# A two-layer hybrid decoder: the mixers' input projected un-normed, 1/rms applied where the slabs are drained

## The reference, cut to what matters

```python
def rms_norm(x, g):
    y = x * rsqrt(mean(x * x, axis=-1, keepdims=True) + 1e-6)
    return y * g
for l in range(DEPTH):
    h = rms_norm(x, norm_mix[l])
    x = x + hybrid_mixer(h, w_in[l], w_out[l], ...)   # split_cols(h @ w_in) feeds three mixers
    h = rms_norm(x, norm_ffn[l])
    x = x + peer_ffn(h, ...)                          # 8 heads x 16 rows of peer_u and peer_v per token
return rms_norm(x, norm_final)
```

## Time and profile before

| | |
|---|---|
| median of 3 runs | 3553.36 us (3552.85 to 3555.71) |
| the profiled execution | 3554.43 us, its span 3552.6 us |
| busy: TensorE / VectorE / ScalarE / GpSimd | 81% / 62% / 21% / 34% of the span |
| projections and mixers | about 0 to 430 and 1780 to 2200 us |
| expert stages | about 430 to 1780 and 2200 to 3545 us |
| moved by DMA | 1243.73 MB, mean 350 GB/s |

### The profile page before, as it was taken

One profiled execution on the slowest core, in us unless ns is written; L12 is line 12 of the kernel. 1 busy time (PEld: TensorE's weight loads), 2 busy tenths in 40 slices (PEclk: granted clock), 3 DMA queues, 4 the chain that ended last, 5 costly groups with the idle time before them and its releaser, 6 DMA issues.

```text
span 3552.6 us, 31376 instructions
## 1 busy us (share of the span) xinstructions
PE 2862.2 (81%) x10451; PEld 1655.6 (47%) x10451; DVE 2199.6 (62%) x3084; ACT 758.4 (21%) x1195; POOL 1219.7 (34%) x1028
## 2 busy tenths in 40 slices
PE   7999948877787788777789999478778878887776
PEld 7888833423342343222388887334234323432322
DVE  6775576565665656555566655765666556655655
ACT  4354411111111111111143544111111111111111
POOL 0000065444444444444400000644444444444442
PEclk9999969999999999999999999799999999999999
DMA  5445599999999999999944454999999999999998
GB/s 192 137 151 165 179 362 420 419 421 421 421 420 422 421 420 411 422 420 419 399 144 137 146 191 153 397 420 419 421 421 421 420 422 421 416 415 422 416 421 341
DMA packets 239647, 1243.73 MB, mean 350 GB/s; under 512 B 24680, under 2 KB 33072, under 8 KB 107440
## 3 DMA queue, kind: packets, MB, share of 16 engines
q0 software_dynamic: 147456, 1073.81, 73.0%
q1 hardware_dynamic: 92080, 168.51, 14.0%
HBM read 1240.14 MB, written 2.10 MB: 350 GB/s over the span
## 4 chain that ended last, share of the span: by engine, by line
DMA 47%; PE 37%; DVE 6%; issue 5%; DVEq 2%; ACT 1%; POOL 1%; SPq 0%; POOLq 0%; ACTq 0%
DMA work<-in_peer_v_dram,idx_v 43%; PE PS L508 17%; PE PS L859 17%; DMA work<-in_peer_u_dram,idx_u 4%; DVE work L1880 2%; DVE xs L1906 1%; POOL work L1252 1%; DVEq L1496 1%; ACT hi L936 1%; DVE lo L1385 1%; PE PS L628 1%; PE PS L606 0%; PE PS L618 0%; DMA gain<-in_w_in_dram 0%; PE PS L794 0%
## 5 line engine op out<-in xcount | busy, mean ns | idle before, releaser
L859 PE MATMUL PS<-work,diag 128*128 128x512 f32 x3968 | 1861.4, 617 | 620.4 <-DMA work<-in_peer_v_dram,idx_v 454.5
L1880 DVE CUSTOM_DVE_ANT_0 work<-work,hn 128x2048 f32<-128x2048 f32 x512 | 1170.3, 2292 | 829.4 <-DMA work<-in_peer_u_dram,idx_u 817.6
L859 PEld LDWEIGHTS PS<-work,diag 128*128 128x128 f32 x3968 | 742.0, 195 | 1710.2 <-issue 1346.0
L1252 POOL DMA_INDIRECT work<-in_peer_u_dram,idx_u x512 | 649.9, 1269 | 1165.1 <-DVEq L1852 896.0
L1252 POOL DMA_INDIRECT work<-in_peer_v_dram,idx_v x512 | 569.6, 1113 | 1136.6 <-PE PS L859 1017.7
L1183 ACT ACTIVATE diag<-cst,act_k 128x128 f32<-128x128 f32 x496 | 185.5, 397 | 1219.9 <-PE PS L859 1209.9
L508 PE MATMUL PS<-hT_hi,hi 128*128 128x256 f32 x960 | 287.6, 300 | 24.5 <-DVE lo L1724 14.1
L508 PE MATMUL PS<-hi,hT_hi 128*128 128x512 f32 (+1 forms) x704 | 276.0, 392 | 3.7 <-DVE lo L1385 3.7
L508 PE MATMUL PS<-hT_lo,hi 128*128 128x256 f32 x960 | 275.7, 287 | 0.0
L508 PE MATMUL PS<-hT_hi,lo 128*128 128x256 f32 x960 | 275.5, 287 | 0.0
L508 PE MATMUL PS<-hi,hT_lo 128*128 128x512 f32 (+1 forms) x704 | 269.6, 383 | 0.0
(11 more groups left out here) (264 smaller groups left out, 1700.5 us busy)
## 6 DMA issues: line engine op xcount, KB each, us to landing
raw<-in_w_in_dram SPq DMA_DIRECT2D x40, 1024.0 KB
gain<-in_w_in_dram SPq DMA_DIRECT2D x38, 1024.0 KB, 5.0
raw<-in_peer_query_dram SPq DMA_DIRECT2D x24, 1024.0 KB
raw<-in_w_out_dram SPq DMA_DIRECT2D x16, 1024.0 KB
gain<-in_w_out_dram SPq DMA_DIRECT2D x16, 1024.0 KB, 5.1
work<-in_peer_query_dram SPq DMA_DIRECT2D x8, 1024.0 KB, 7.7
work<-in_peer_u_dram,idx_u POOLq DMA_INDIRECT x512, 11.6
work<-in_peer_v_dram,idx_v POOLq DMA_INDIRECT x512
```

The costliest lines, as they stand in the source:

```text
L859: mm = pe.matmul(PS[:, j, :], diag[:, n % RING, :], vrow[n % RING][:, j * 512:(j + 1) * 512], start=(k == 0), stop=(k == (TOPK - 2 if last ...
L1252: pool.indirect_dma_start(out=dst, out_offset=None, in_=tables[table], in_offset=bass.IndirectOffsetOnAxis(ap=idx, axis=0)).then_inc(loade ...
L1880: dve.tensor_tensor_reduce(r, r, hn[:, b, :], 1.0, 0.0, ALU.mult, ALU.add, pre[:, b, k:k + 1]).then_inc(u_free.sem, 1)
```

## The change

hn is no longer the normed input but tokens times gain, without 1/rms (`weigh_inputs`), so that it can be turned before the sums of squares are known. Since the projection is linear in each token, 1/rms enters at the drain. Slabs whose tokens lie on partitions (kv, q, ih, vm, gh, om) get it as ScalarE's scale, one activation for each block of tokens in place of one for both. Slabs whose tokens lie along the free axis (fh, qh, qkm0, qkm1) are multiplied by a row of 1/rms on VectorE (`scale_rows`); fh and qh then go through ScalarE's sigmoids and silu in place. For the row, VectorE makes two diagonals (`lay_rstd`), TensorE spreads them over all partitions by two matmuls after piece 2 (`spread_rstd`), and ScalarE copies the result out.

Tiles are turned ahead of the piece that needs them: piece p waits for tile 4 + p alone, tiles 4 and 5 are turned before piece 0, tiles 6 and 7 before piece 1, and the convolution weights after piece 1. In layer 0 SP issues the gain first, block 0 of the tokens in halves, then block 1, and piece 1 ahead of the constants and small loads. Between the layers tiles 0 to 3 are turned one of TensorE's rows earlier, block 1 is weighed slab by slab behind each part of `take_last_sum`, and the splits of pieces 1 and 2 come ahead of tiles 6 and 7 and of the root. After the last layer the final norm is as before.

The diff, cut (the end of the program, the new wait before a slab's first piece, and the remaining drains, which change as kv does, are left out):

```diff
+ROWS_SCALED = ["fh", "qh", "qkm0", "qkm1"]
+DRAINED = [name for name, _, _ in SLABS if name not in ("qkm0", "qkm1")]
+ND = len(DRAINED)
...
+            sp.dma_start(gain[:].unsqueeze(1), layer_of(norm_mix, 0).partition_broadcast(P)).then_inc(gain_loaded.sem, 16)
+            for i in range(2):
+                half = slice(i * D // 2, (i + 1) * D // 2)
+                sp.dma_start(xs[:, 0, half], x[0, 0:P, half]).then_inc(x_loaded[i].sem, 16)
+            sp.dma_start(xs[:, 1, :], x[0, P:SEQ, :]).then_inc(x_loaded[2].sem, 16)
...
-                stop_until(sp, "sp", vidx_ready.sem, vidx_ready.upto(l, 0))
-                sp.dma_start(gain[:].unsqueeze(1), layer_of(norm_mix, l).partition_broadcast(P)).then_inc(gain_loaded.sem, 16)
+                if l > 0:
+                    stop_until(sp, "sp", vidx_ready.sem, vidx_ready.upto(l, 0))
+                    sp.dma_start(gain[:].unsqueeze(1), layer_of(norm_mix, l).partition_broadcast(P)).then_inc(gain_loaded.sem, 16)
...
                 load_piece(0)
                 if l == 0:
+                    sp.wait_ge(turned.sem, turned.upto(l, 4))
+                    load_piece(1)
...
                 load_piece(2)
-                stop_until(sp, "sp", turned.sem, turned.upto(l, 4))
-                load_piece(1)
+                if l > 0:
+                    stop_until(sp, "sp", turned.sem, turned.upto(l, 4))
+                    load_piece(1)
...
+                def spread_rstd():
+
+                    pe.wait_ge(rstd_diag.sem, rstd_diag.upto(l, 1))
+                    for b in range(NB):
+                        mm = pe.matmul(PS[:, 6, b * P:(b + 1) * P], ones[:], diag[:, b, :], start=True, stop=True)
+                    mm.then_inc(rstd_spread.sem, 1)
...
-                for f in range(4, 8):
-                    turn_mix(l, f)
-                pe.wait_ge(turned_dve.sem, turned_dve.upto(l, 8))
-                if l == 0:
-                    pe.wait_ge(consts_loaded.sem, 16)
+                def conv_step():
+                    pe.wait_ge(turned_dve.sem, turned_dve.upto(l, 8))
+                    conv_weights()
+
+                steps[0] = nothing
+                steps[1] = conv_step
+                steps[2] = spread_rstd
                 for p in range(IN_PIECES):
+                    if p < 2:
+                        for f in range(4 + 2 * p, 6 + 2 * p):
+                            turn_mix(l, f)
+                    if p < 4:
+
+                        pe.wait_ge(turned_dve.sem, turned_dve.upto(l, 5 + p))
+                    if l == 0 and p == 8:
+                        pe.wait_ge(consts_loaded.sem, 16)
                     if p % 4 == 0 and p >= 8:
-
-                        pe.wait_ge(drained.sem, drained.upto(l, p // 4 - 1))
+                        slab_free(p // 4 - 2)
                     project(l, p)
                     steps.get(p, nothing)()
...
-                    if l + 1 < DEPTH and k in (6, 8, 10, 12):
-                        turn_mix(l + 1, (k - 6) // 2)
+                    if l + 1 < DEPTH and k in (4, 6, 8, 10):
+                        turn_mix(l + 1, (k - 4) // 2)
...
+            def square_sums(l, b):
+
+                if l == 0:
+                    for i in ((0, 1) if b == 0 else (2,)):
+                        act.wait_ge(x_loaded[i].sem, 16)
+                if b == 0 or l == 0:
+                    unread = squares[:, b, :] if l == 0 else lo[1][:].bitcast(F32R)
+                    a = act.activation(unread, xs[:, b, :], ACT.Square, accum_out=ss[:, b:b + 1])
+                else:
+                    for o in range(NO):
+                        act.wait_ge(x1_final.sem, x1_final.upto(l - 1, o + 1))
+                        a = act.activation(squares[:, 1, o * 512:(o + 1) * 512], xs[:, b, o * 512:(o + 1) * 512], ACT.Square,
+                                           accum_out=ssq[:, b, o:o + 1])
+                a.then_inc(sumsq_ready.sem, 1)
+
+            def root(stage):
+
+                act.wait_ge(var_ready.sem, stage)
+                act.activation(rms[:], ss[:], ACT.Sqrt).then_inc(std_ready.sem, 1)
...
+            take_mix(0, range(5))
             round_piece(0, 0)
-            take_mix(0, range(8))
+            take_mix(0, range(5, 6))
+            square_sums(0, 0)
+            square_sums(0, 1)
+            round_piece(0, 1)
+            take_mix(0, range(6, 8))
+            root(1)
+            round_piece(0, 2)
...
+                    both = lambda f: [f(b) for b in range(NB)][-1]
+                    if name in ROWS_SCALED:
+                        act.wait_ge(scaled.sem, scaled.upto(l, ROWS_SCALED.index(name) + 1))
                     if name == "fh":
-                        act.activation(cum, pt, ACT.Sigmoid)
-                        a = act.activation(kk, pt, ACT.Sigmoid, scale=-1.0)
+                        act.activation(kk, cum, ACT.Sigmoid, scale=-1.0)
+                        a = act.activation(cum, cum, ACT.Sigmoid)
                     elif name == "qh":
-                        a = act.activation(silq, pt, ACT.Silu)
+                        a = act.activation(silq, silq, ACT.Silu)
                     elif name in ("qa0", "qa1"):
                         c = 512 * int(name[2])
-                        a = act.activation(qraw[:, :, c:c + 512], p, ACT.Copy)
+                        a = both(lambda b: act.activation(qraw[:, b, c:c + 512], p[:, b, :], ACT.Copy, scale=rstd[:, b:b + 1]))
                     elif name == "kv":
-                        act.activation(gnat[:], p[:, :, 256:256 + 2 * NH], ACT.Copy)
-                        a = act.activation(kvraw, p[:, :, 0:256], ACT.Copy)
-                    elif name in ("qkm0", "qkm1"):
-                        m = 4 * int(name[3])
-                        a = act.activation(cin[:, m:m + 4, :], pt, ACT.Copy)
...
+                round_to(5)
+                act.wait_ge(rstd_spread.sem, rstd_spread.upto(l, 1))
+                act.activation(rstd_row, PS[:, 6, 0:SEQ], ACT.Copy).then_inc(rstd_laid.sem, 1)
                 drain(0)
...
+                    act.activation(rms[:], ones[:, 0:NB], ACT.Sqrt)
+                    act.wait_ge(x0_final.sem, x0_final.upto(l, 1))
+                    square_sums(l + 1, 0)
+                    diagonals(HEADS - 1, 1, range(8, TOPK, 2), last=True)
+                    take_mix(l + 1, range(6))
                     round_piece(l + 1, 1)
+                    round_piece(l + 1, 2)
+                    take_mix(l + 1, range(6, 8))
+                    square_sums(l + 1, 1)
+                    root(var_ready.upto(l, 2))
...
+            def weigh_inputs(l, b, o, n):
+
+                cols = slice(o * n, (o + 1) * n)
+                dve.tensor_tensor(hn[:, b, cols], xs[:, b, cols], gain[:, cols], ALU.mult).then_inc(normed.sem, 1)
+
+            def lay_rstd():
+
+                for b in range(NB):
+                    d = dve.tensor_scalar(diag[:, b, :], ident, rstd[:, b:b + 1], None, ALU.mult)
+                d.then_inc(rstd_diag.sem, 1)
...
+            dve.wait_ge(gain_loaded.sem, gain_loaded.upto(0, 16))
+            for o in range(2):
+                dve.wait_ge(x_loaded[o].sem, 16)
+                weigh_inputs(0, 0, o, D // 2)
+            take_mix(0, range(2))
+            dve.wait_ge(x_loaded[2].sem, 16)
+            weigh_inputs(0, 1, 0, 512)
+            take_mix(0, range(2, 4))
+            weigh_inputs(0, 1, 1, 512)
+            take_mix(0, range(4, 5))
+            split_piece(0, 0)
+            take_mix(0, range(5, 6))
+            weigh_inputs(0, 1, 2, 512)
+            weigh_inputs(0, 1, 3, 512)
+            dve.drain().then_inc(gain_used.sem, 1)
+            split_piece(0, 1)
+            take_mix(0, range(6, 8))
+            variance(None, 2)
             invert(None, 1)
-            normalise(0, 0)
-            normalise(0, 1)
-            take_mix(0, range(4))
-            split_piece(0, 0)
-            take_mix(0, range(4, 8))
+            lay_rstd()
+            split_piece(0, 2)
...
+                def scale_rows(name, dst):
+
+                    j = [n for n, _, _ in SLABS].index(name)
+                    dve.wait_ge(pieces_used.sem, pieces_used.upto(l, 4 * (j + 1)))
+                    dve.tensor_tensor(dst, pair(j).rearrange("p b (m t) -> p (b m) t", m=2),
+                                      bc(rstd_row.unsqueeze(1), [P, 4, SEQ]), ALU.mult).then_inc(scaled.sem, 1)
+                    dve.drain()
...
                 split_to(6)
+                dve.wait_ge(rstd_laid.sem, rstd_laid.upto(l, 1))
+                scale_rows("fh", cum)
...
-                split_to(9)
+                split_to(10)
+                scale_rows("qh", silq)
                 dve.wait_ge(drained.sem, drained.upto(l, 2))
-                split_to(10)
...
+                scale_rows("qkm0", cin[:, 0:4, :])
                 soft(0)
                 for n in range(NBATCH):
                     take_probs(n)
                     if n + 1 < NBATCH:
                         soft(n + 1)
```

(79 more changed lines are left out.)

89 lines of the change are left out of this document (47 added, 42 removed).

## The result

The changed kernel takes 3567.07 us (median of 7 runs, 3565.75 to 3568.05), the kernel before, run beside it, 3555.16 (7 runs). The ratio is 1.0034, 95% interval 1.0024 to 1.0043: 12 us slower, where the prediction said 3555.7 and no change. The profiled execution has a span of 3565.3 us, against the 3552.6 of the earlier trace rows.

A forecast was written before the change was run, and what follows sets the result against it. Up to and in the recurrence's levels, the chain VectorE and ScalarE share sets the time, not the products. Layer 0 summed to 0.0 and layer 1 to +2.3: 3553.36 + 2.3 = 3555.7 us, range 3549.5 to 3560.

The forecast's parts named there:

- Start of layer 0: Layer 0's projection start: first product at 18.8 against 24.82; with added TensorE work, -5.6 us at the end of fh.
- Between the layers: From last expert row to layer 1's projection: first product 5.7 us earlier, -3.3 at the end of fh after added costs.
- x: Delay of the last expert row by piece 1's earlier load: between 0 and 2.7 us, taken as +1.2.
- The fh and qh drains: VectorE's row products ahead of ScalarE's drains: first level weights +4.8 us after fh, taken as +4.6 in each layer.
- costed at nothing: Row products on qkm slabs, 1.22 us each, and remaining doubled drains: free where TensorE is never idle.
- Drains by scale: ScalarE's kv and q drains, two activations for one: 1.2 us each instead of 0.6 and 0.9, +1.0 per layer.
- The rival of the clock: In the recurrence's levels, gaps make TensorE's clock fall again: +6 on top of +2.3, 3561.7 us; chance 0.12.
- rival that the start's gain stands: Up to the levels TensorE's queue is last, hiding fh and qh products: -8.5, 3544.9 us; chance 0.15.

The follow-up runs named there:

- before, a wait that is always met: Kernel before, with a second wait on ScalarE's own finished rounding added after TensorE's wait, ahead of its fh and qh drains: 3555.53 us.
- before, load on TensorE's wait: Kernel before, with an always-met second wait written ahead of TensorE's wait at fh and qh, so the table load carries TensorE's wait: 3560.89 us.
- one wait: Changed kernel, with ScalarE waiting at fh and qh for VectorE's row product alone, its wait for TensorE removed: 3559.83 us.
- waits swapped: Changed kernel, with ScalarE's two waits before fh and qh kept but in the other order, so the table load carries TensorE's wait: 3559.43 us.
- product first: Changed kernel, with VectorE multiplying fh and qh by the row of 1/rms before it splits pieces 5 and 9: 3560.52 us.
- four repairs: Changed kernel, with ScalarE's TensorE wait dropped, row products before splits, turns two rows later, and layer 0's piece 0 rounded and split before tile 4: 3554.13 us.
- fh and qh unscaled: Changed kernel, with 1/rms left out of fh and qh, which ScalarE takes straight from PSUM as in the kernel before: 3552.13 us.
- run with the later turns: Changed kernel, with tiles 0 to 3 turned between the layers two rows later again, as in the kernel before: 3566.58 us.

## Why the prediction was wrong

*Start of layer 0: mechanism right, size off by 1.5.* First product at 20.28, not 18.8. The prediction kept piece 0's rounding at 14.55, because four 1 MB blocks lie ahead of it in both orders; it began at 15.91. Of these 1.4, the transfer of piece 0 is 0.8 (15.35 above, when nothing stands in front) and tile 4's rounding on ScalarE about 0.6.

*Between the layers: right.* -5.8 for -5.7, and x was 1.22 for 1.2, in all runs with the early turns. By the rule of the Trainium skill ("DMA: Bandwidth & Descriptors", Queues, rings and completion order), which I had read as giving 2.7 here, the load would have had its full share before the last row; the row shows less than half of that.

*The fh and qh drains: the step that failed.* It priced them at +4.8 by the first weights; measured is 34.0 - 26.5 = +7.5. The difference of 2.7 is twice the 1.28 load. The step counted the exponential's load as "in series", because the trace of before shows it there, and left those of sigmoid and silu at nothing, because there they lay in idle time. They aren't in its list "costed at nothing" either, where the cover would have had to be named: the load was free as long as nothing made it wait for VectorE. With the table loads repaired the step holds. End of fh to first weights, in both layers:

```
before                               26.5
before, a wait that is always met    26.5
before, load on TensorE's wait       27.8
after, in two executions             34.0
one wait                             31.3
waits swapped                        31.3
product first                        30.6
four repairs                         28.3
fh and qh unscaled                   26.5
```

Loads out of the open: 2.7 (2 x 1.28 = 2.56). Product first: 3.4 (2.29 + 1.25 = 3.54). Both and no more: 5.7 (6.1). After with hidden loads against fh and qh unscaled: 4.8, where the sum had 4.8. TensorE's waits ahead of pieces 7 and 8 in layer 1 are 1.75 and 1.46 after, for 0.9 and 1.6 predicted; with the loads hidden they are 0.86 and 1.46.

*Drains by scale: mechanism right, a little too dear.* kv and the gates' columns take 1.0 up to the next rounding (1882.99 to 1884.00) and q 1.14 (1909.72 to 1910.86), where the prediction had 1.2 for each. Before, the same stretches took 0.54 and 0.91, so the rows say +0.7 per layer for the predicted +1.0, and the levels, in which both drains stand, are longer by 1.0 and 0.7 in the two layers. The run without them gained 3.4 us over two layers; the intervals leave both 2.0 and 1.4 open.

*The rival of the clock* (0.12): the clock fell more often, but the levels aren't longer by it. Table by stretches, the levels of layer 1 before, then the 22 us ahead of them and the levels after (window, length, busy PE, PEld, DVE, ACT, POOL, granted clock, DMA share, GB/s):

```profile
1845.96:1909.96 64.00, 59.93 (x341) 51.98 (x340) 42.84 (x45) 24.84 (x21) 0.00 (x0) 0.95 0.45 148
```
```profile
1824.86:1846.86 22.00, 18.59 (x151) 18.01 (x151) 15.88 (x23) 10.58 (x9) 0.00 (x0) 1.00 0.27 77
1846.86:1910.86 64.00, 57.78 (x329) 51.30 (x328) 39.28 (x43) 27.14 (x26) 0.00 (x0) 0.91 0.46 149
```

The 22 us ahead of the levels have gaps of 3.4 in all, the waits ahead of pieces 7 and 8 among them. The levels behind have a granted clock of 0.91 instead of 0.95. One minus the clock times the length is the work, at full speed, that the lower clock takes away. Summed over the levels and the 20 us behind them in both layers it is 11.8 to 12.2 in the three executions with the change's drains as they are, 8.4 without the factor on kv and q, 3.8 with one wait, 8.3 with the waits swapped, and 5.2 to 7.0 in the three of the kernel before and its variants. So TensorE lost some 6 us more to 1.2 instead of 2.4 GHz. The time from the first to the last level's weights doesn't follow: it is 62.5 and 63.0 in the two layers after, 62.2 and 64.2 with one wait, which has the smallest loss of these, and without the factor on kv and q 61.7 and 62.1, as short as before (61.6 and 62.3) at a larger loss. In the levels VectorE and ScalarE's chain ends last, as the prediction said, and a slower TensorE beside it cost nothing that these traces show. So the clock doesn't explain why the medians give back 8.1 and 8.5 with one wait and with swapped waits where the timeline gives back 5.3 (2.7 in each layer); that difference of about 3 is what the intervals leave open.

*The sum.* Predicted +2.3, the table loads +5.1, the start of layer 0 +1.5: 8.9 of 12. Most of the rest, 2.7 in the profiled executions, lies behind the levels, where the prediction had nothing. Of it, 0.95 is shown: in layer 1 ScalarE idles 6.71 instead of 5.46 for a load of w_out, and TensorE idles for the split behind it, 0.95 in this execution, 0.58 to 1.08 in all ten traces of the changed kernel and its variants and not at all in the three of the kernel before and its variants. What causes the remainder stays open; that stretch differs by up to 4.8 between traces (290.0 to 294.8 in layer 0). The rival that the start's gain stands fell with the row-first run: the chain and not TensorE's queue is last. The chance of 0.12 for slower was too low: the range's upper end counted the drains' chain at most 5 in each layer, and a bound for work that is inserted into a wait should have held every instruction that can be pushed behind that wait.

## What to carry to other kernels

When a drain gets a new producer, list everything that stood in the idle time ahead of it, table loads included, and ask of each which wait it will carry. If an activation needs two waits and a table, look at the compiled order: write last the wait that is met first, or drop the one that the other implies. Multiply before you split: the producer's step on which another engine waits goes ahead of work that fits into that engine's answer (2.3 and 1.25 us here). Gains at a stage's start are kept only as far as the chain behind them isn't lengthened: here 5.5 us gained were outweighed by 15.8 lost behind them.

## What the runs showed of the hardware

The table load took 1.28 us (mean 1283 ns in the groups by line) at every place, and where nothing else held the activation, it followed 0.02 after the load's end (1823.18 + 1.28, next 1824.48). The Trainium skill ("ScalarE: Activation LUTs", What ACT_TABLE_LOAD costs) puts a further 1380 ns of drain beside these 1283. The trace doesn't show that part: where the load lay in the open here, its price in the timeline was the load alone, 1.3 a piece.

In the first 8 us of layer 1's projection the granted clock lay between 0.63 and 1.00 over the profiled executions, and at 0.79 and 1.00 in two of the kernel before that differ in nothing but a wait that is always met. The first piece took 6.1 and 7.6 in these two. At 0.63 the work taken away is 8 x 0.37 = 3 us, about a quarter of what was to be explained here, and all that follows in the layer moves with it. It is why the drains were measured from the end of fh. The record of the clock can miss such a stretch: in layer 0 of the run with the later turns it reads 1.00 over these 8 us, but the matmuls at its start follow each other by 0.21 us, where they follow by 0.12 at full clock, and the first piece took 9.3, more than the 8.8 and 8.9 of the two executions of the changed kernel that read 0.68 and 0.67.
